# A two-block transformer kernel: loading the opening by pairs of K tiles, products of constants in three waits, and column quarters for the sums of squares in two seams

## The reference, cut to what matters

```
def rmsnorm(x, g):
    xf = x.astype(jnp.float32)
    y = xf * lax.rsqrt(jnp.mean(xf * xf, axis=-1, keepdims=True) + EPS)
    return (y * g.astype(jnp.float32)).astype(x.dtype)
...
    h = h + rmsnorm(mix, g[1])
    ff = conv_ffn(rmsnorm(h, g[2]), ffn_w_up[l], ffn_conv[l], ffn_w_down[l])
    h = h + rmsnorm(ff, g[3])
```

## Time and profile before

| | |
|---|---|
| median of three runs | 3402.62 us (3402.41 to 3402.77) |
| the profiled execution | 3403.99 us |
| its span, first to last instruction | 3402.2 us |
| TensorE busy | 3368.2 us (99%) |
| VectorE, ScalarE, GpSimd busy | 74%, 51%, 3% |
| mean granted TensorE clock | 0.998 of full speed |

### The profile page before, as it was taken

How to read it: one execution, slowest core, us unless ns; L and a number is a source line. 1 busy time by engine, 2 the same in 40 slices (tenths; PEclk the granted TensorE clock), 3 DMA queues, 4 the chain that set the end, 5 groups by cost and what they waited for, 6 DMA issues and landing times. The chain is left out here.

```text
span 3402.2 us, 65679 instructions
## 1 busy us (share of the span) xinstructions
PE 3368.2 (99%) x25119; PEld 3148.3 (93%) x25119; DVE 2510.4 (74%) x3658; ACT 1726.2 (51%) x2638; POOL 109.9 (3%) x100
## 2 busy tenths in 40 slices
PE   9999999999999999999999999999999999999998
PEld 8998899989998989898899889999999998899987
DVE  6886888887887778787788865656785367767863
ACT  4563655545554545454555545556555344555552
POOL 0100202000200100000002000000000000000000
PEclk9999999999999999999999999999999999999999
DMA  4333223332333322222133321212223221123232
GB/s 142 111 101 113 91 87 105 106 112 96 101 105 107 106 81 81 81 78 97 63 106 105 118 100 63 69 62 69 100 94 105 94 75 38 44 75 100 93 105 81
DMA packets 89676, 311.33 MB, mean 92 GB/s; under 512 B 10816, under 2 KB 15296, under 8 KB 89472
## 3 DMA queue, kind: packets, MB, share of 16 engines
q1 hardware_dynamic: 89056, 307.19, 27.1%
q0 software_dynamic: 416, 1.29, 0.1%
HBM read 306.34 MB, written 2.10 MB: 91 GB/s over the span
## 5 line engine op out<-in xcount | busy, mean ns | idle before, releaser
L892 PE MATMUL ps<-x_hi,w_hi 128*128 128x264 f32 (+2 forms) x1840 | 572.8, 311 | 2.6 <-ACT pair L2880 0.9
L892 PE MATMUL ps<-x_hi,w_lo 128*128 128x264 f32 (+2 forms) x1840 | 562.9, 306 | 0.0
L892 PE MATMUL ps<-x_lo,w_hi 128*128 128x264 f32 (+2 forms) x1840 | 561.9, 305 | 0.0
L892 PE MATMUL ps<-h_hi,w_hi 128*128 128x264 f32 (+3 forms) x1282 | 406.0, 317 | 4.2 <-DVE h_lo L3205 1.9
L892 PE MATMUL ps<-h_hi,w_lo 128*128 128x264 f32 (+3 forms) x1282 | 395.2, 308 | 0.0
L892 PE MATMUL ps<-h_lo,w_hi 128*128 128x264 f32 (+3 forms) x1282 | 394.4, 308 | 0.0
L892 PEld LDWEIGHTS ps<-x_hi,w_hi 128*128 128x128 f32 x1840 | 347.1, 189 | 32.0 <-issue 10.2
L892 PEld LDWEIGHTS ps<-x_hi,w_lo 128*128 128x128 f32 x1840 | 347.9, 189 | 14.7
L892 PEld LDWEIGHTS ps<-x_lo,w_hi 128*128 128x128 f32 x1840 | 346.3, 188 | 15.8
L2989 DVE TENSOR_TENSOR w_lo<-raw,w_hi 128x1024 fp32r<-128x1024 f32 x214 | 259.8, 1226 | 111.7 <-ACT w_hi L1839 107.9
L993 PE MATMUL ps<-t_hi,w_hi 128*128 128x256 f32 x1152 | 322.7, 280 | 0.0
(11 more groups left out here) (421 smaller groups left out, 8796.5 us busy)
## 6 DMA issues: line engine op xcount, KB each, us to landing
raw<-wstream SPq DMA_DIRECT2D x577, 512.0 KB, 3.3
res<-xT SPq DMA_DIRECT2D x8, 256.0 KB, 7.4
out<-res SPq DMA_DIRECT2D x8, 256.0 KB, 2.4
near_bias<-consts POOLq DMA_DIRECT2D x1, 512.0 KB, 4.4
g_chunk<-consts POOLq DMA_DIRECT2D x1, 264.0 KB, 3.3
g_keep<-consts POOLq DMA_DIRECT2D x1, 256.0 KB, 3.1
par<-params SPq DMA_DIRECT2D x1, 232.5 KB, 7.6
far_bias<-consts POOLq DMA_DIRECT2D x1, 128.0 KB, 3.9
```

Of the source, the lines that this page charges most:

```text
L892: m = pe.matmul(ps[:, bank, 0:n], w[:, slot, wt, :], x[:, k, c0:c0 + n], start=first and q == 0, stop=last and q == 2)
```

## The change

Three independent parts.

- The weight stream is laid out anew for units 0 to 3: each of the four loads now holds two K tiles of all four units. The first is loaded in two halves, x by pairs of K tiles (the first pair by token halves). ScalarE and VectorE split a pair at a time, and TensorE's new `opening` goes pair by pair over both token halves, with all four units side by side. The idle run has 4 products for 6.
- `keep_warm` multiplies the constant matrix by columns of the parameter table, into columns of a bank that nothing reads: five products in the seam before hgrn, two and three in hgrn's end.
- In the seams with four late tiles, four squares at a time are multiplied by quarters (32 columns) of the constant matrix into four partition quarters of a bank, at steps 21 and 27, and in the second half before K tile 3's low products and after all of them. ScalarE then copies the bank, scaled by 32, and one more product sums the quarters (`mean_of`). In the seams with one late tile the squares come four at a time as well, with the whole matrix, at step 19 and after the steps.

```
-IDLE = 6
+IDLE = 4
...
+    opening = units[:RING].reshape(RING, P, KD // 2, 2, P)
+    units[:RING] = opening.transpose(2, 1, 3, 0, 4).reshape(RING, P, KD, P)
...
             for h in range(2):
+                sp.dma_start(res[:, 0:2, tokens(h)], x_in[:, 0:2, HALF * h:HALF * (h + 1)]).then_inc(s_x[h][0], 16)
+                if h == 0:
+                    sp.dma_start(raw[:, 0, 0:RING], wstream[0][:, 0:RING]).then_inc(s_front, 16)
+                    sp.dma_start(raw[:, 0, RING:KD], wstream[0][:, RING:KD]).then_inc(s_load[0], 16)
+            for pair in range(1, KD // 2):
+                sp.dma_start(raw[:, pair], wstream[pair]).then_inc(s_load[pair], 16)
+                sp.dma_start(res[:, 2 * pair:2 * pair + 2, META:T], x_in[:, 2 * pair:2 * pair + 2, :])\
+                    .then_inc(s_x[0][pair], 16)
...
+            def keep_warm(bank, n, start):
+
+                for _ in range(n):
+                    pe.matmul(ps[:, bank, S - SPARE:S], mean_w[:, :], par[:, 0:SPARE], start=start, stop=True,
+                              skip_group_check=True)
...
+            def opening(st):
...
+                for pair in range(KD // 2):
+                    tiles = range(2 * pair, 2 * pair + 2)
+                    for h in range(2):
+                        pe.wait_ge(s_xhi, 4 * pair + 2 * h + 2)
+                        for k in tiles:
+                            if k == 0 and h == 0:
+                                pe.wait_ge(s_front, 18)
+                            elif h == 0:
+                                pe.wait_ge(s_lo, pair + 1)
+                            for j in range(RING):
+                                product(h, j, k, w_hi, hi, k == 0 and h == 0, False)
+                                product(h, j, k, w_lo, hi, False, False)
+                        pe.wait_ge(s_xlo, 4 * pair + 2 * h + 2)
+                        for k in tiles:
+                            for j in range(RING):
+                                m = product(h, j, k, w_hi, lo, False, k == KD - 1)
+                                if h and k == KD - 1:
+                                    m.then_inc(s_unit, 1)
...
-                square_steps = (17, 19, 21) if halved == 1 else range(18, 18 + KD)
+                square_steps = {19: 0} if halved == 1 else {21: 0, 27: 1}
...
+                                if h and st.get("outs") and halved > 1 and steps == 30:
+                                    mean_of(st, 0)
...
-                    between.append(lambda: squares_of(st, 1, range(KD)))
+                    if halved == 1:
+                        between[0] = lambda: [squares_of(st, 1, b) for b in range(KD // SQUARES)]
+                    else:
+                        between[3] = lambda: squares_of(st, 1, 0)
+                        between[KD] = lambda: squares_of(st, 1, 1)
+                        between[KD + 1] = lambda: mean_of(st, 1)
...
+                pe.wait_ge(s_sqr, st["s0"] + KD * h + SQUARES * (block + 1))
+                for j in range(SQUARES):
+                    rows = slice(FG * j, FG * j + FG)
+                    m = pe.matmul(ps[rows, 2 + h, 0:st["tok"] // 2], mean_w[:, rows],
+                                  square_buffer(st, h, SQUARES * block + j), start=block == 0,
+                                  stop=block == KD // SQUARES - 1, skip_group_check=True)
+                m.then_inc(s_sqp, SQUARES)
+
+            def mean_of(st, h):
+
+                pe.wait_ge(s_ms, means_of(st, h) + 1)
+                pe.matmul(ps[:, 2 + h, 0:st["tok"] // 2], mean_w[:, :], part_buffer(st, h), start=True, stop=True)\
+                    .then_inc(s_ms, 1)
...
             def renorm(st):
-                squares_of(st, 0, range(SQUARES, KD))
-                between.append(lambda: squares_of(st, 1, range(KD)))
+                squares_of(st, 0, 1)
+                keep_warm(7, 5, True)
+                between[0] = lambda: [squares_of(st, 1, b) for b in range(KD // SQUARES)]
...
                 begin(nxt, 1, range(0, 3))
+                keep_warm(0, 2, False)
                 turn_and_score(KD - 1)
                 begin(nxt, 1, range(3, 4))
+                keep_warm(0, 3, False)
                 state_steps(KD - 1)
...
+            def mean_square(st, h):
...
+                act.wait_ge(s_sqp, st["s0"] + KD * (h + 1))
+                act.activation(part_buffer(st, h), ps[:, 2 + h, 0:st["tok"] // 2], ACT.Copy, scale=float(FG))\
+                    .then_inc(s_ms, 1)
+                return s_ms, means_of(st, h) + 2
```

More of the change, by code:

```diff
@@ L55 @@
 FG = 32
+SPARE = 224
 FB = 5
@@ L199, in project2 @@
     def project2(units, chunks, lead, tok, after, *outs, early=0):
[L201 removed]
+        counts = dict(v=1, a=2 * KD, **inputs(*outs))
+        if outs and LATE[len(chunks)] > 1:
+            counts["o"] = 4
+        down("project2", units, chunks, lead, counts=counts, after=after, outs=outs,
              tok=tok, early=early)
@@ L931, in first_units @@
                 order = [(k, j) for g in first for k in range(KD) for j in g]
-                if st["t0"] and before(st).get("scaled") and st["held"] == 1:
+                if before(st).get("scaled") and st["held"] == 1:
                     order = [(k, j) for k in range(KH) for j in range(3)] + [(k, 3) for k in range(KH)] + \
                         [(k, j) for k in range(KH, KD) for j in range(4)]
-                ahead = (KD // 2 if st["kind"] == "glu2" else 0) if between else KD
                 hi, lo = x_src
@@ L954, in first_units @@
                 for k in range(KD):
[L955 to L958, removed]
+                    if k in between:
+                        between.pop(k)()
                     pe.wait_ge(s_xlo, x0 + k + 1)
@@ L1857, in load, with slice_of, high_x @@
                 load_silu()
[L1858 to L1868, removed]
+                def slice_of(pair, k):
+                    return raw[:, pair, RING * k:RING * (k + 1)], w_hi[:, 0:RING, 2 * pair + k, :]
+                def high_x(h, pair):
+                    k, c = 2 * pair, half_cols(S, h)
+                    if h == 0 or pair == 0:
+                        act.wait_ge(s_x[h][pair], 16)
+                    act.activation(x_hi[:, k:k + 2, c], res[:, k:k + 2, c], ACT.Copy).then_inc(s_xhi, 2)
+                high_x(0, 0)
+                act.wait_ge(s_front, 16)
+                src, dst = slice_of(0, 0)
+                act.activation(dst, src, ACT.Copy).then_inc(s_front, 1)
+                act.wait_ge(s_load[0], 16)
+                src, dst = slice_of(0, 1)
+                act.activation(dst, src, ACT.Copy).then_inc(s_hi, 1)
+                high_x(1, 0)
+                for pair in range(1, KD // 2):
+                    act.wait_ge(s_load[pair], 16)
+                    act.activation(paired(w_hi, pair), paired_raw(pair), ACT.Copy).then_inc(s_hi, 1)
+                    high_x(0, pair)
+                    high_x(1, pair)
             def glu(st):
@@ L3007, in load, with low_x, low_slice @@
             def load(st):
[L3008 to L3020, removed]
+                dve.memset(idle[:, :], 0.0).then_inc(s_set, 1)
+                dve.memset(eps[:, 0:1], EPS).then_inc(s_set, 1)
+                def low_x(h, pair):
+                    k, c = 2 * pair, half_cols(S, h)
+                    dve.wait_ge(s_xhi, 4 * pair + 2 * h + 2)
+                    dve.tensor_tensor(x_lo[:, k:k + 2, c], res[:, k:k + 2, c], x_hi[:, k:k + 2, c].bitcast(F32),
+                                      ALU.subtract).then_inc(s_xlo, 2)
+                def low_slice(k):
+                    return dve.tensor_tensor(w_lo[:, 0:RING, k, :], raw[:, 0, RING * k:RING * (k + 1)],
+                                             w_hi[:, 0:RING, k, :].bitcast(F32), ALU.subtract)
+                dve.wait_ge(s_front, 17)
+                low_slice(0).then_inc(s_front, 1)
+                low_x(0, 0)
+                dve.wait_ge(s_hi, 1)
+                low_slice(1).then_inc(s_lo, 1)
+                low_x(1, 0)
+                for pair in range(1, KD // 2):
+                    dve.wait_ge(s_hi, pair + 1)
+                    dve.tensor_tensor(paired(w_lo, pair), paired_raw(pair), paired(w_hi, pair).bitcast(F32),
+                                      ALU.subtract).then_inc(s_lo, 1)
+                    low_x(0, pair)
+                    low_x(1, pair)
             def glu(st):
```

102 lines of the change are left out of this document (57 added, 45 removed).

## The result

| | before | after |
|---|---|---|
| median (19 runs each) | 3402.78 us (3402.1 to 3405.68) | 3410.94 us (3406.84 to 3412.07) |
| the profiled execution, its span | 3403.99, 3402.2 us | 3409.8, 3408.0 us |
| ratio after to before | | 1.0021, 95% interval 1.0015 to 1.0028 |

What follows compares the result with a forecast made beforehand. TensorE, busy for 99% of the span, was taken to bound the kernel. Opening -1.3, quarters +1.2, products of constants and one-late-tile seams 0, clock +1.7 gave +1.6, so 3404.2 us, range 3399.5 to 3408.0.

Steps and rivals of the forecast that it cites:

- Clock: Behind three new TensorE waits, in the opening and two quartered seams: one half-rate fall counted as likeliest, +1.7 us.
- All fall: Rival: the clock falls behind all three new waits, 5.1 instead of 1.7 us, so 3407.6 us; chance 8%.
- Quarters: Two seams with four late tiles: squares by column quarters make the second half start 0.6 us later each, +1.2 together.
- the chain of hand-overs: Quartered seams' second half: block 1, copy and mean in a row at the end, root at 2356.9 where it was 2356.31.
- The block: Four squares multiplied by quarters in a seam: 0.65 us taken, bounds 0.44 and 1.78.
- the prediction's estimate of 0.56: Time in us of a block of four quarter products, by the skill's speedup share, before the changes of form.
- Opening: Start of the kernel: first product at 6.0, unit 4 at 32.15, a gain of 1.3 us (bounds 1.7 and 0.1).
- Costs nothing unless the clock then rises later: Condition on the opening's idle run, cut from 12 records in 5.33 us to 8 in about 3.6.
- Products of constants: Filling waits in hgrn's end and the seam before hgrn: counted as 0, bounds 0 and -1.7 us.
- one-late-tile seams: Seams with one late tile: the same eight products with the same waits, forecast 0, within 0.2 us.
- The sum: All terms added: -1.3 + 1.2 + 0 + 1.7 = +1.6 us, so 3404.2 us.

Runs made afterwards that it cites:

- e2: The changed kernel with the two quartered seams put back to eight products one by one; 3403.94 us, ratio 1.0002 to the kernel before.
- e4: The changed kernel with first-half mean at step 28, second-half block 1 and mean ahead of K tiles 6's and 7's low products; 3405.78 us, ratio 1.0003.
- e5: The changed kernel with six idle products ahead of the first load in place of four; 3409.17 us, ratio 1.0014 to the kernel before.
- e6: The changed kernel without the ten products of constants in hgrn and the seam before it; 3411.34 us, ratio 1.0023 to the kernel before.
- e7: The changed kernel with quarters only in the two seams' first half, mean at step 28, second-half squares one by one; 3403.77 us, ratio 1.0000.
- e11: The changed kernel profiled once more, nothing altered; single time 3406.95 us.
- e3: The changed kernel with the opening's last pair of K tiles run unit by unit, both halves of each; 3405.70 us, ratio 1.0005 to the kernel before.
- e10: The kernel before the change profiled once more, nothing altered; single time 3403.56 us.
- e1: The changed kernel with products of constants put into TensorE's three new waits (opening, two quartered seams); 3405.41 us, ratio 1.0004 to the kernel before.
- e8: The changed kernel with e3's opening order, e5's six idle products and e7's first-half quarters together; 3397.51 us, ratio 0.9983 to the kernel before.
- e9: As e8, but without quarters: both halves' squares one by one as in e2; 3399.54 us, ratio 0.9988 to the kernel before.

## Why the prediction was wrong, point by point

**Clock: the step that failed.** "I take one of the three as the likeliest number", with 8% for *All fall*. The step that failed is this count: one fall was put into the sum, where the traces have 2.6 in the mean. Behind that stood a wait of 2.19 with a fall and one of 1.65 without. In the profile after all three fell, at 1.51, 1.53 and 1.53 in the stretches behind them (table; forecast 1.7 each). Over all traces in which such a wait stands unfilled: behind the opening's 3.1 us 7 falls of 7 (after, e2, e4, e5, e6, e7, e11), behind the seams' 2.1 8 of 10 (after, e3, e5, e6, e11). Behind the 1.6 of e4's seams there are 0 of 2, behind the 1.65 before fox_values 0 of 13. Counting gives 1 + 0.8 + 0.8 = 2.6 falls, 4.0 us where the sum had 1.7.

The Trainium skill (TensorE: Matmul & The Clock Gate, "Why this matters for your kernels") warns against idle gaps of TensorE between bursts of products, and the gaps that it names are longer than the seams' 2.1 us. The opening's 7 of 7 agree with it; the seams' 8 of 10 come behind shorter waits than it names, and there the measurement decides.

The wait of 2.19 before hgrn has, with e10 and e6, one fall in three, and a fall costs nothing there: with the fall and without it, the root before hgrn and that of hgrn's end are 300.52 and 300.51 us apart (before, e10). So the prediction's price of nothing for that place was right.

**Quarters: a term of the right sign, mis-sized.** +0.6 a seam was forecast, +1.4 measured (28.94 for 27.56, 28.53 for 27.10). In the first half the prediction let the mean product follow ScalarE's copy, with the root at 2339.5; the mean product waited for TensorE to reach step 30, 0.67 behind that copy, and the root came at 2340.01. Counted from the root at 2328.75 (2328.88 after), the first product came 0.38 earlier, not 0.8. The mean at step 28 brings the rest (e4, e7). In the second half the chain of hand-overs was right in kind, 17.8 from first product to first product for 17.45 forecast and 16.05 before. (The working's steps there add to a root at 2356.8 where it says 2356.9; that changes little.) From the last square to the root it took 3.05 where before took 1.30. e4 wins 0.97 of that back by putting block 1 ahead of the last low products, behind which it had stood 1.14 from the last square on; the other 0.78 is the copy and the mean themselves, and goes only with the quarters (e7, 1.28). The block was sized well, 0.69 for 0.65. The Trainium skill (TensorE: Matmul & The Clock Gate, "Measured speedup vs the span model") gives 2.38 times for three column tiles. Four took 0.69 here in place of four times 0.445, 2.6 times: less than the 3.2 times in the prediction's estimate of 0.56, but with the changes of form in it.

**Opening: right in the profile, too good for the median.** There it gave -1.35 (forecast -1.3), at the price of the fall, +1.5. "Costs nothing unless the clock then rises later" was the condition that failed elsewhere. With four idle products the opening has half-rate products ahead of 12 us in e1, e3, e4, e6 and e7, and in after, e2 and e11 not; with six (e5, e8, e9) in none. The kernel before has six as well and a half rate at 9.7 and 8.4, but it waits for x in its opening, up to 9.2 and 9.0. Among the openings that differ in nothing else, unit 4 starts at 32.10 to 32.60 (after, e2, e11) or at 33.99 to 34.59 (e4, e6, e7), where before had 33.45 and 33.30. That also fits the 1.1 us by which the median after stands above its profile.

Three executions against eight suggest that the idle run decides this, and do not settle it. A rival is not separated, the landing of the first load's second half: ScalarE takes it up at 5.2 to 5.9 in after, e2 and e11, and at 6.2 to 6.7 in e3, e4, e6 and e7, though at 5.5 in e1, and at 6.5 in e9, which has six idle products and the full rate.

**Products of constants and one-late-tile seams: right.** Zero forecast. Without the products of constants the ratio is 1.0023 for 1.0021 (e6), no difference within 3 us. From the first root to the last in the seam before fox_values it takes 21.69 us after and 21.81 before, and in the seam before hgrn 16.75 and 16.74.

**The sum.** Opening -0.1 (the mean of the six unit-4 times, 33.3, against 33.4), falls +4.0, seams +2.8: +6.7, inside the interval of 5.1 to 9.5. Of the 5.1 between this and the forecast's +1.6, the falls are 2.3, the seams 1.6 and the opening 1.2. The rival that came true is *All fall*, on top of a seam twice as dear. That rival's 3407.6, and the upper end of the range, are three falls beside the forecast seams and opening. The prediction also took 0.2% for about the least that can be told from none; the interval of the ratio here, 1.0015 to 1.0028, tells it. What stays open is what makes a fall happen in one execution and not in another.

## What to carry to other kernels

A wait of 2 to 3 us that an edit opens on the busiest engine is not only its own length: count a fall behind it as likely (15 of 17 here for the two new kinds of wait, 1.5 us each; one of three for the old one before hgrn; none for the single waits of 1.6 to 1.7 in the seams), and fill the wait or remove it before counting the edit's gain. If a batched order makes all results end together, let the last batch run result by result (e3): the first follower's chain then runs under the rest. A reduction that saves the busiest engine work but adds hand-overs belongs where other work covers them (the first half here), not at the end of a chain.

## What was unexpected of the hardware

The half rate is not a property of the program alone: two executions of one kernel, with the same wait to 0.01 us, differ in it (e10, e11). It does not need one long wait either: in fox_values two waits of 1.3 and 0.9 us close together have a fall behind them in ten traces of thirteen, where a single one of 1.65 before that stage has none in any. A fall costs 1.4 to 1.6 us by the means in four places, and nothing in the seam before hgrn (300.52 and 300.51), where by the prediction's working ScalarE's squares come last.
